# A hybrid decoder layer on one core: feed-forward by seven block products, in three token passes

## The reference

```python
z = rmsnorm(x, g_mix) @ w_in                     # (1024, 4112): u, q, k, v, r, a_low, gate_s5, gate_gla
o5 = z5 * sigmoid(z5 @ w_s5_glu)                 # z5 = gelu(S5 scan of u)
merged = sigmoid(gate_s5) * (o5 @ w_s5_br) + sigmoid(gate_gla) * (og @ w_gla_br)
x = x + merged @ w_out
h2 = rmsnorm(x, g_ffn)
x = x + jnp.square(jax.nn.relu(h2 @ w_ff1)) @ w_ff2   # w_ff1 (1024, 4096), w_ff2 (4096, 1024)
y = rmsnorm(x, g_final)
```

## Time and profile before

| | |
|---|---|
| median of 3 runs | 2862.91 us |
| the profiled execution, its span | 2858.6 us |
| TensorE matmul busy | 2810.9 us (98%), 16170 matmuls |
| VectorE, ScalarE, GpSimd busy | 1324.5, 502.5, 1165.6 us |
| feed-forward of half 0 | about 713 to 1421 us |
| feed-forward of half 1 | about 2110 to 2847 us |

### The profile page before, as it was taken

How to read it: one execution, slowest core, us unless ns; L and a number is a source line. 1 busy time by engine, 2 the same in 40 slices (tenths; PEclk the granted TensorE clock), 3 DMA queues, 4 the chain that set the end, 5 groups by cost and what they waited for, 6 DMA issues and landing times.

```text
span 2858.6 us, 40302 instructions
## 1 busy us (share of the span) xinstructions
PE 2810.9 (98%) x16170; PEld 2529.5 (88%) x16170; DVE 1324.5 (46%) x2039; ACT 502.5 (18%) x731; POOL 1165.6 (41%) x917
## 2 busy tenths in 40 slices
PE   6999999999999999999999999999999999999998
PEld 4778887888888888888899999999999999999997
DVE  8845657364433333233723555666444223332235
ACT  4222231412100000001232232142120000000002
POOL 3434432545444444444434332244444434344441
PEclk9999999999999999999999999999999999999999
DMA  4323244531111111113113332563211111111112
GB/s 146 122 93 89 67 133 155 188 100 52 48 48 48 48 48 48 45 48 108 56 49 121 81 83 92 176 218 100 68 45 48 45 49 45 49 45 45 48 45 80
DMA packets 123118, 230.33 MB, mean 81 GB/s; under 512 B 15408, under 2 KB 43856, under 8 KB 122832
## 3 DMA queue, kind: packets, MB, share of 16 engines
q1 hardware_dynamic: 79440, 150.16, 17.1%
q10 hardware_dynamic: 43520, 77.83, 8.6%
HBM read 183.85 MB, written 44.09 MB: 80 GB/s over the span
## 4 chain that ended last, share of the span: by engine, by line
PE 95%; DVE 3%; DMA 1%; DVEq 1%; ACT 0%; issue 0%; ACTq 0%
PE ps L594 29%; PE ps L592 29%; PE ps L593 29%; PE ps L771 1%; PE ps L856 1%; PE ps L889 1%; PE ps L883 1%; PE ps L802 0%; PE ps L780 0%; DMA s_constants<-f_m 0%; DVE f_m L1675 0%; PE ps L813 0%; DMA f_h<-xT 0%; DVE f_g L1675 0%; DVE f_h L1675 0%; PE ps L987 0%
## 5 line engine op out<-in xcount | busy, mean ns | idle before, releaser
L571 POOL TENSOR_TENSOR w_hi<-w_raw,zero 128x512 fp32r<-128x512 f32 x456 | 534.2, 1172 | 1590.3 <-PE ps L594 1564.1
L592 PE MATMUL ps<-r_h,w_hi 128*128 128x352 f32 (+1 forms) x2352 | 817.5, 348 | 8.2 <-DVE r_h L1675 6.8
L594 PE MATMUL ps<-r_h,w_lo 128*128 128x352 f32 (+1 forms) x2352 | 816.4, 347 | 0.0
L593 PE MATMUL ps<-r_o,w_hi 128*128 128x352 f32 (+1 forms) x1968 | 678.8, 345 | 0.0
L573 POOL TENSOR_TENSOR w_lo<-w_raw,w_hi 128x512 fp32r<-128x512 f32 x456 | 633.3, 1389 | 64.7
L592 PE MATMUL ps<-r_z,w_hi 128*128 128x352 f32 (+1 forms) x1440 | 515.6, 358 | 0.0
L594 PE MATMUL ps<-r_z,w_lo 128*128 128x352 f32 (+1 forms) x1440 | 513.9, 357 | 0.0
L593 PE MATMUL ps<-r_h,w_hi 128*128 128x512 f32 (+1 forms) x1352 | 499.5, 369 | 0.0
L592 PEld LDWEIGHTS ps<-r_h,w_hi 128*128 128x128 f32 x2352 | 442.9, 188 | 45.2 <-issue 11.0
L594 PEld LDWEIGHTS ps<-r_h,w_lo 128*128 128x128 f32 x2352 | 443.0, 188 | 32.2
L593 PE MATMUL ps<-r_m,w_hi 128*128 128x352 f32 (+1 forms) x1240 | 421.1, 340 | 0.0
(11 more groups left out here) (323 smaller groups left out, 2395.6 us busy)
## 6 DMA issues: line engine op xcount, KB each, us to landing
w_raw<-wpack SPq DMA_DIRECT2D x456, 256.0 KB, 2.6
f_z<-s_constants ACTq DMA_DIRECT2D x16, 514.0 KB, 4.8
f_h<-s_constants ACTq DMA_DIRECT2D x16, 514.0 KB, 4.9
f_h<-xT ACTq DMA_DIRECT2D x16, 512.0 KB, 4.6
gate_s_scratch<-f_m ACTq DMA_DIRECT2D x8, 528.0 KB, 3.5
gate_gla_scratch<-f_m ACTq DMA_DIRECT2D x8, 528.0 KB, 3.7
f_z<-gate_s_scratch SPq DMA_DIRECT2D x8, 528.0 KB, 4.9
f_o<-xT ACTq DMA_DIRECT2D x4, 1040.0 KB, 7.9
```

The lines of the kernel that those rows point to most:

```text
L571: pool.tensor_tensor(w_hi[:, s, :], raw, zero[:, :].to_broadcast([P, WB]), ALU.subtract)
L592: pe.matmul(out, wh, h, start=first, stop=False)
L593: pe.matmul(out, wh, l, start=False, stop=False)
L594: return pe.matmul(out, wl, h, start=False, stop=last)
```

## The change

- The feed-forward of both halves moves behind both mixers. It runs over all 2080 tokens in three passes, with twice 348, 348 and 344 tokens. Within a pass each of the two products (up and down) is a 2x2 block product: halves of the features of the weights, and the two halves of the pass's tokens as columns. It is made by Strassen's seven products of sums of blocks.
- An *item* of a pass is one hidden tile quad of an up (`("up", q)`, 16 of them) or one pair of output tiles of a down (`("down", g, d)`, 16): seven products, each with one 128x512 block of weights (sums of blocks for four of them) and 12 matmuls, in the order 1, 5, 6, 2, 7, 3, 4. Products 1, 6, 7 and 4 go into one PSUM bank, 5 and 3 into a second, 2 into a third; the bank is read between them, so that the partial sums become the four results. The banks take turns by a plan (`plan_banks`).
- Sums of hidden blocks and of token blocks are made on VectorE (`hidden_mix`, `token_mix`), their high parts on ScalarE, their low parts on VectorE (`hidden_low`, `token_low`). The hidden squares move to ScalarE.
- The weight sums are made once, by 128 DMAs of 512 KB each within DRAM that GpSimd issues during the mixers (`sum_dma`); half of them add to what is in the destination. Before each new stage of a batch GpSimd waits for all earlier ones.
- In the feed-forward the weights' high parts move from GpSimd to ScalarE (`weight_high`), GpSimd makes the low parts alone, and there are four raw buffers.
- x after the mixers is stored to DRAM (`x1_dram`) with the roots, and comes back for passes 1 and 2. The input norm of half 1 moves into half 0's output projection (`first_out`). The final norm of pass p is made in pass p + 1 (`y_square`, `y_add`, `y_scale`); that of the last pass at the end (`end_square`, `end_sum`, `end_scale`).
- The feed-forward is written out on all engines.

The core of the diff:

```diff
-SETS = {"q": (1, 1), "gate": (1, 1), "out": (4, 4), "ff": (48, 48)}
+PASSES = 3
+HALF_TOKENS = [348, 348, 344]
+ORDER = [1, 5, 6, 2, 7, 3, 4]
+ITEMS = ([("up", 0), ("up", 1), ("up", 2), ("down", 0, 0), ("down", 0, 1)]
+         + [item for g in range(1, FF_GROUPS)
+            for item in ([("up", q) for q in (2 * g + 1, 2 * g + 2) if q < QUADS] + [("down", g, 0), ("down", g, 1)])])
...
             def sum_dma(stage, unit, which):
+                elif stage == 1:
+                    pool.dma_start(sums(0) if which == 0 else sums(2), blocks(4) if which == 0 else blocks(3),
+                                   accum_op=ALU.add).then_inc(sums_made, 16)
...
+            for f in range(PASSES * PASS_BLOCKS):
+                s = f % RING
+                pool.wait_ge(w_high, f + 1)
+                pool.tensor_tensor(w_lo[:, s, :], raw(s), w_hi[:, s, :].bitcast(F32), ALU.subtract
+                                   ).then_inc(w_split[s], 1)
...
+            def up_product(p, item, j):
+                if v in (1, 5, 2):
+                    bank_free((p, item, 0, name))
+                elif v == 6:
+                    pe.wait_ge(first_copied, 3 * use + 1)
+                elif v == 7:
+                    pe.wait_ge(first_copied, 3 * use + 3)
+                elif v == 3:
+                    pe.wait_ge(first_copied, 3 * use + 2)
+                else:
+                    pe.wait_ge(pairs_read, dve_reads(p, item) + 2)
+                pe.wait_ge(w_split[s], (HALVES * MIXER_BLOCKS + f) // RING + 1)
...
+            def down_product(p, item, j):
+                for z in range(2):
+                    if v in (1, 5, 2):
+                        bank_free((p, item, z, name))
+                    elif v == 6:
+                        pe.wait_ge(pairs_read, reads + 1 + z)
+                    elif v == 7:
+                        pe.wait_ge(pairs_read, reads + 5 + z)
+                    elif v == 3:
+                        pe.wait_ge(pairs_read, reads + 3 + z)
+                    else:
+                        pe.wait_ge(pairs_read, reads + 9 + z)
...
+            def weight_high(f):
+                s = f % RING
+                act.wait_ge(w_landed[s], 16 * (W_LANDED[s] + f // RING + 1))
+                act.wait_ge(w_used[s], (HALVES * MIXER_BLOCKS + f) // RING)
+                act.activation(w_hi[:, s, :], raw(s), ACT.Copy).then_inc(w_high, 1)
...
+            def up_sum(p, item, out, t, name):
+                tt(fv(hid_lo(q, out), n), fv(F_T[t], n), ps[:, BANK[p, item, 0, name], 0:n], ALU.add).then_inc(pairs_read, 1)
+            def relu(p, q, v, op, t):
+                h = fv(hid_lo(q, v), HALF_TOKENS[p])
+                dve.scalar_tensor_tensor(h, h, 0.0, root_of(p, t), op, ALU.mult).then_inc(relu_ready, 1)
+            def hidden_low(p, q, part):
+                v, count = ((1, 2), (5, 2), (2, 2), (4, 1))[part]
+                tt(some(ra, hid_lo(q, v), count, n), some(fa, hid_lo(q, v), count, n),
+                   some(ra, hid_hi(q, v), count, n).bitcast(F32), ALU.subtract).then_inc(v_low, 1)
```

More of the change, by code:

```diff
@@ L214 @@
 ANGLES = 9
[L217 removed]
+SETS = {"q": (1, 1), "gate": (1, 1), "out": (4, 4)}
 SET_BASE, SET_TOTAL = {}, [0, 0]
@@ L239, with norm_lo, norm_hi, hid_lo @@
 PI2_1, PI2_2, PI2_3 = 6.28125, 0.0019350051879882812, 3.019916050e-07
[L242 to L258, removed]
+FH = 1
+F_X = X_HI[FH]
+SLOT_LO = [WORK[FH] + 7 * SB * s for s in range(3)]
+SLOT_HI = [X_LO[FH] + 7 * SB * s for s in range(3)]
+F_T = [WORK[FH] + 21 * SB + SB * x for x in range(3)]
+F_TOTAL = X_LO[FH] + 21 * SB
+F_SQ = A_G
+F_ROOT = [A_E, A_E, A_E]
+Y_ROOT = A_G
+RAW_MORE = A_G + W
+def norm_lo(k, v):
+    if v == 4:
+        return F_X + k * W + 2 * SB
+    return (QKV if k < 2 else SIDE)[FH] + 12 * SB * (k % 2) + SB * BLOCK_AT[v]
+def norm_hi(k, v):
+    if v == 4:
+        return F_X + (k + 4) * W + 2 * SB
+    return norm_lo(k, v) + 6 * SB
+def hid_lo(q, v):
+    return SLOT_LO[q % 3] + SB * BLOCK_AT[v]
+def hid_hi(q, v):
+    return SLOT_HI[q % 3] + SB * BLOCK_AT[v]
+def item_at(p, item):
+    return p * PASS_BLOCKS + ITEMS.index(item) * STEPS7
+def up_count(p, q):
+    return p * QUADS + q
+def down_count(p, g, d):
+    return (p * FF_GROUPS + g) * 2 + d
+def dve_reads(p, item):
+    n = p * (4 * QUADS + 28 * FF_GROUPS)
+    for other in ITEMS[:ITEMS.index(item)]:
+        n += 4 if other[0] == "up" else 14
+    return n
+SUMS_AFTER = [("up", 0), ("up", 1)]
+SUMS_STEP = [3, 3]
+SUM_OF = {5: 0, 6: 1, 7: 2, 3: 3}
+SUM_STAGES = 6
+SUM_BATCH = 4
+SUM_DMAS = 8 * 2 * FF_GROUPS
+Y_TILES = [0, 4, 1, 5, 2, 6, 3, 7]
+SCALE_FROM = 5
+END_SQ = [QKV[FH], QKV[FH] + 4 * SB]
+NORM_BASE = [0, 16, 30]
+FULL_BASE = [0, 16, 32]
+T_BASE = [0, 16, 24]
+X_LANDED = [48 if m % X_PIECE == 0 else 16 for m in range(KT_D)]
+W_LANDED = [HALVES * MIXER_BLOCKS // RAW if s < RAW else 0 for s in range(RING)]
 class Arena:
@@ L656, in first_pair @@
             def first_pair(half, stage, it, split, hi, lo, between=None):
-                alone = split == SP_H2 or (split == SP_X and half > 0)
+                alone = split == SP_X and half > 0
                 for s in range(1 if alone else 2):
@@ new lines, in first_copy @@
+            def first_copy(p, item, j):
+                use = up_count(p, item[1])
+                x, name, reads = ((0, "a", 1), (2, "c", 2), (1, "a", 3))[j]
+                if use:
+                    before = p, item
+                    if item[1]:
+                        before = p, ITEMS[max(i for i in range(ITEMS.index(item)) if ITEMS[i][0] == "up")]
+                    else:
+                        before = p - 1, ("up", QUADS - 1)
+                    act.wait_ge(pairs_read, dve_reads(*before) + reads)
+                n = HALF_TOKENS[p]
+                act.activation(fv(F_T[x], n), ps[:, BANK[p, item, 0, name], 0:n], ACT.Copy).then_inc(first_copied, 1)
@@ L2334, in _ @@
                     s5_tables()
-                else:
-                    at = QKV[half] + Q_V
-                    for k in range(KT_D):
-                        last = norm_add(NORM[half - 1]["y"], ft(half - 1, at), ft(half - 1, at, 1 + (k - 1) % 3), k)
-                        if k and k < KT_D - 1:
-                            last.then_inc(sq_used, 1)
-                    output_scale(half - 1)
                 gate_sums(half)
@@ L2421, in _ @@
[L2421 to L2433 removed]
+                if half == 0:
+                    first_out()
+                else:
+                    second_out()
```

1170 lines of the change are left out of this document (837 added, 333 removed).

## The result

The changed kernel takes **2990.06 us** (median of 4 runs, 2982.31 to 2993.41) against 2861.65 us (2860.22 to 2866.39) for the kernel before on the same chip: the ratio is 1.044, 95% interval 1.0423 to 1.0457. I had forecast 2788 us, between 2712 and 2885, and faster; 2990 lies above the range and above every rival (B, the highest, at 2899). The span of the profiled execution is 2980.5 us, 121.9 us longer than before.

A forecast was written before the change was run, and what follows sets the result against it. TensorE, busy for 98% of the span, was taken to bound the kernel. 2858.6 - 174.2 (matmuls) + 90 (stalls) + 5 (DMAs) + 4 (end) = 2783.4 us profiled, so 2788 us as median; range 2712 to 2885.

The forecast's parts named there:

- B: Feed-forward: the port shared by VectorE and GpSimd sets the pace, making the kernel slower, 2899 us; chance 0.24.
- matmuls: Feed-forward: fewer, narrower matmuls take 1270.4 us instead of 1444.6, so -174.2 us.
- stalls inside the passes: Feed-forward: TensorE waits on VectorE's queue, 62 us in the passes, 2.6 us per two ups and two downs.
- around the pass changes: Between passes: preparing next tokens, square sums and scalings join VectorE's queue; 28 us taken, 20 us each worked out.
- GpSimd's DMAs: Mixers: 128 weight-sum DMAs issued by GpSimd, with waits for groups ahead of weight splits; +5 us, bounds 0 and some 30.
- moved input norm and the rest of the mixers: Half 1's input norm in half 0's output projection, hidden (17 against 22 us), 10 us if loading twice as slow; x1 stores free.
- end: After the last product: 17.5 us instead of 13.9 for additions, sums, roots, scalings and store; +4 us.
- the slope: Matmul pace from 512 and 352 columns: 0.44 ns per column, giving 0.1581 us at 348 columns and 0.1564 at 344.
- the walk: VectorE's feed-forward order followed: 40 us per pass, 120 in all, plus 40 between passes; upper bound 160 us.
- three stalls of a group: Two ups and two downs: TensorE waits 1.7 us in up after up, 1.3 and 1.6 us in down after up.
- I take somewhat above half: Feed-forward stalls set between 0 and 160 us: 62 in the passes and 28 between them, +90 us.
- Rival C: Mixers: GpSimd's DMAs hold back the weight splits, 30 us instead of 5, total 2813 us; chance 0.06.

The follow-up runs named there:

- e_order: Changed kernel with the same work, but VectorE's mixes and low parts behind the additions in downs after ups, ScalarE's hidden high parts shifted: 2873.86 us.
- GpSimd's cut: GpSimd's feed-forward low parts over 128 of 512 columns, in the kernel with both the semaphore for the drain and the new VectorE and ScalarE order: 2780.54 us.
- e_nosum: Changed kernel without any weight sums, plain blocks loaded where the sums were: 2909.93 us, ratio 1.0169 to the kernel before.
- e_low128: Changed kernel with GpSimd's feed-forward low parts over 128 of 512 columns only: 2863.92 us, ratio 0.9999 to the kernel before.

## Why the prediction was wrong

Term by term, in the order of the sum:

| term | forecast | measured |
|---|---|---|
| matmuls | -174.2 | about -169 |
| stalls inside the passes | 62 | 112 |
| around the pass changes | 28 | 82, and 12 at the first start, 5 at the end |
| GpSimd's DMAs | +5 | +72 (drain 60, DMAs 12) |
| moved input norm and the rest of the mixers | 0 | +18 |
| end | +4 | +4.7 |

The stalls are counted against the forecast's pace, so they hold the 5 us that the matmuls lack, and the 10.3 us that the feed-forward lost before: -174.2 + 112 + 82 + 17 - 10.3 + 72 + 18 + 4.7 = 121.

- **The matmuls were right.** A stretch without a gap has 350/2202 = 0.1589 us per matmul at 348 columns (e_order above), against 0.1581 from the slope: 5376 x 0.0008 = 4.3 us, and a little for the 344.
- **The walk had the right mechanism and was still too small, and I did not believe even that much.** It had put the three stalls of a group at 4.7 us, and the trace has 1.25 + 1.55 + 1.52 at these very products. For the 18 groups and three first downs, where 112 us came, it has 94; the other 26 of its 120 are the first and the last ups of the passes, which the table counts with the starts, the changes and the end. The step that failed is the sentence "I take somewhat above half", with its reason that "each stall of TensorE also gives VectorE time to catch up". VectorE had caught up anyway: in the second down of each group it has only additions and pauses between them, so every group starts clean, just as the walk did, and loses the same. An average under 1 says that the loss does not grow; it doesn't say that it is small.
- **Around the pass changes the walk was shorter still**: 20 us each, 29 with the ups beside them, 41 measured. It had the right queue. It left out that the collisions at the port also stretch the final norm and the token blocks (14 to 17 us of the 41 went with GpSimd's cut), and the granted clock (0.86), which I had nowhere in the sum although hold only for a TensorE that never pauses.
- **The DMAs: the wait that I looked for was not the one that came.** I counted issue time (51 us; measured 0.71 us for a plain and 1.15 to 1.24 for an adding one, so about 122) and the waits for groups, and stopped there. I had counted what stands ahead of the splits in GpSimd's queue, and had not read the instruction between the two parts of a split: a drain, whose cost of 0.15 us in the trace before held only for a GpSimd that has issued no DMA. The bound of "0 and some 30 us" was therefore no bound. Rival C named the right place (weight splits held back by GpSimd's DMAs) and priced it at 30 instead of 72.
- Beside C the prediction cited the Trainium skill ("SBUF — State Buffer", SBUF: two separate sides): VectorE in a 2-port mode keeps GpSimd from writing descriptors. That isn't what the drain shows, which ends with the landing. One of its longest holds falls in a stretch in which VectorE does nothing, here GpSimd's timeline and a window over the hold:

```profile
828.27 1.23 POOL L818 DMA_DIRECT2D down_sums<-wpack  x1
829.06 1.50 POOL L799 TENSOR_TENSOR w_hi<-w_raw,zero 128x512 fp32r<-128x512 f32 x1
838.11 1.28 POOL L801 TENSOR_TENSOR w_lo<-w_raw,w_hi 128x512 fp32r<-128x512 f32 x1 [7.54 <-issue]
...
830.60:838.00 7.40, 7.40 (x35) 6.71 (x34) 0.00 (x0) 2.34 (x4) 0.00 (x0) 0.77 0.70 162
```

- **Moved input norm: not hidden.** I compared durations (17 against 22 us) and left out two queues: VectorE's square sums stand ahead of its first output tile (a gap of 4.35 us), and TensorE's sum over partitions stands in TensorE's own queue (5.50 us), so anything late there is paid in full, with the clock behind it.
- **Rival B** gave 2899 us from a port that sets the pace. The feed-forward's loss is B's in size (161 + 40 us, 200.8 measured), but that is chance: its mechanism is refuted by e_order, where with all of GpSimd's work on the port the group runs at the matmuls' pace. The right picture was the forecast's own walk, with sizes above its upper bound.

All that I had bounded came out above its upper bound: the feed-forward's stalls at 200.8 us against 160, the DMAs at 72 against 30, the moved norm with the rest of the mixers at 18 against 10.

## What to carry to other kernels

When a walk through an in-order queue finds a stall, check whether the queue is empty at the start of each period: if it is, the walk repeats, and its number is the forecast, not its upper end (here it was even somewhat low). Before issuing DMAs from an engine that also computes, look in its code for drains; a semaphore raised by the one instruction that is needed waits for that alone. In a queue that shares a port put what another engine waits for ahead of what may be late: here that was worth 116 us, with no instruction less (collisions avoided included).

## What the runs showed of the hardware

- A drain on GpSimd behind a DMA that it has issued ends when that DMA has landed: from issue to the next instruction 4.40 us (landing 4.2) for plain copies and 8.3 (7.7) for adding ones of 512 KB within DRAM; without a DMA it costs 0.15 us, and with a semaphore instead the same DMAs hold up nothing.
- An adding DMA within DRAM takes 7.7 us for 512 KB at the median where a copy takes 4.2, and its issue 1.15 to 1.24 us of GpSimd instead of 0.71 to 0.75.
- Stretches at the 1.2 GHz level followed pauses of TensorE, short ones too: the granted clock was 0.83 in 640 to 680 of e_nosum with gaps of 4.35 and 5.50 us, 0.86 in the pass change of after, and in after also 0.53 in 1172.4 to 1176.0 behind a gap of 2.22 us and 0.52 in 1486.3 to 1489.7 behind one of 2.41 us. It stayed at 1.00 in 1924 to 1940 with a gap of 3.35 us, and in 1540 to 1900, where the pauses are of 1.3 to 1.6 us. So the length of the gap alone doesn't tell it here.
- The shared port: two VectorE mixes of 348 columns with both inputs in SBUF took 1.76 us beside GpSimd's low parts of 512 columns and 0.95 us beside those of 128 (e_low128).
